# Two unrolled layers with constant waits in a two-layer attention, SSD and mixture-of-experts kernel

## What is computed

```
h = rms_norm(x, norm1_g[i])
proj = h @ w_in[i]            # q | k | v | z | xbc | dt | gate_a | gate_m
ya = diff_attention(q, k, v, lam, rel_bias)    # 8 heads, two softmax maps each
ym = ssd_mixer(z, xbc, dt_raw, ...)            # conv of 5, chunked scan both ways
merged = sigmoid(gate_a) * (ya @ w_attn_out) + sigmoid(gate_m) * (ym @ w_ssm_out)
x = x + merged @ w_out[i]
hn = rms_norm(x, norm2_g[i])
x = x + hier_moe(hn, ...)     # top 1 of 4 groups, top 2 of its 8 experts, 32 experts of width 512
```

## Time and profile before

| | |
|---|---|
| median of three runs | 1922.25 us |
| the profiled execution, its own time | 1922.67 us |
| its span in the trace | 1920.6 us |
| PE busy | 1749.7 us, 91% |
| granted TensorE clock, mean | 0.968 |

### The profile page before, as it was taken

One profiled execution on the slowest core, in us unless ns is written; L12 is line 12 of the kernel. 1 busy time (PEld: TensorE's weight loads), 2 busy tenths in 40 slices (PEclk: granted clock), 3 DMA queues, 4 the chain that ended last, 5 costly groups with the idle time before them and its releaser, 6 DMA issues.

```text
span 1920.6 us, 27786 instructions
## 1 busy us (share of the span) xinstructions
PE 1749.7 (91%) x9070; PEld 1094.1 (57%) x9070; DVE 710.0 (37%) x1363; ACT 656.6 (34%) x1318; POOL 666.4 (35%) x536
## 2 busy tenths in 40 slices
PE   6999999998799999998769999999987999999997
PEld 5889766787444343343358897667864433443432
DVE  5528576423321221221255285674232212222211
ACT  4565555754111111111145665557441111111110
POOL 6688655796000000000056886557950000000000
PEclk9999899998899999999989998999988999999999
DMA  6444211455699999999924442114557999999995
GB/s 254 169 176 174 91 45 45 176 221 218 279 421 426 428 427 428 428 428 427 395 97 158 176 176 89 45 45 176 233 205 291 427 428 427 427 429 427 428 427 251
DMA packets 39770, 528.87 MB, mean 275 GB/s; under 512 B 4248, under 2 KB 7064, under 8 KB 7872
## 3 DMA queue, kind: packets, MB, share of 16 engines
q1 hardware_dynamic: 39584, 526.89, 66.7%
q0 software_dynamic: 32, 0.02, 0.0%
HBM read 525.82 MB, written 1.06 MB: 274 GB/s over the span
## 4 chain that ended last, share of the span: by engine, by line
PE 49%; issue 32%; POOL 8%; DMA 5%; DVE 4%; ACT 1%; SPq 0%; POOLq 0%; DVEq 0%; ACTq 0%
PE PS L1038 9%; POOL view L1946 8%; PE PS L721 5%; PE PS L723 5%; PE PS L722 5%; PE PS L1069 5%; DMA view<-in_w_exp_up_dram 5%; PE PS L855 2%; PE PS L815 2%; PE PS L816 2%; PE PS L817 2%; DVE view L1588 2%; PE PS L1019 2%; PE PS L890 1%; PE PS L1004 1%
## 5 line engine op out<-in xcount | busy, mean ns | idle before, releaser
L1946 POOL TENSOR_TENSOR view<-view,view 128x512 fp32r<-128x512 f32 x448 | 578.6, 1314 | 650.1 <-ACT view L1158 645.3
L1038 PE MATMUL PS<-view,view 128*64 128x512 f32 x2048 | 447.7, 593 | 26.7 <-DMA view<-in_w_exp_up_dram 18.1
L1158 ACT ACTIVATE view<-view 128x512 fp32r<-128x512 f32 x448 | 273.6, 628 | 201.0 <-PE PS L723 189.8
L1038 PEld LDWEIGHTS PS<-view,view 128*64 128x64 f32 x2048 | 146.8, 137 | 321.5 <-issue 321.4
L721 PE MATMUL PS<-view,view 128*128 128x512 f32 x704 | 296.3, 421 | 8.9 <-POOL view L1946 7.2
L723 PE MATMUL PS<-view,view 128*128 128x512 f32 x704 | 276.0, 392 | 0.0
L722 PE MATMUL PS<-view,view 128*128 128x512 f32 x704 | 275.8, 392 | 0.0
L1069 PE MATMUL PS<-view,view 128*64 128x512 f32 x1024 | 231.9, 606 | 1.0 <-ACT view L1407 1.0
L1839 DVE TENSOR_TENSOR view<-PS,view 128x512 f32<-128x512 f32 x32 | 22.1, 692 | 486.7 <-PE PS L1019 421.3
L721 PEld LDWEIGHTS PS<-view,view 128*128 128x128 f32 x704 | 133.6, 190 | 47.4 <-POOL view L1946 12.6
L722 PEld LDWEIGHTS PS<-view,view 128*128 128x128 f32 x704 | 133.6, 190 | 32.8 <-issue 8.2
(11 more groups left out here) (241 smaller groups left out, 2055.8 us busy)
## 6 DMA issues: line engine op xcount, KB each, us to landing
view<-in_w_exp_gate_dram SPq DMA_DIRECT2D x64, 2048.0 KB, 19.9
view<-in_w_exp_up_dram SPq DMA_DIRECT2D x64, 2048.0 KB, 22.7
view<-in_w_exp_down_dram SPq DMA_DIRECT2D x64, 2048.0 KB, 25.8
view<-in_w_mix_dram SPq DMA_DIRECT2D x56, 2048.0 KB, 8.0
view<-bias_table SPq DMA_DIRECT2D x2, 1536.0 KB, 11.4
view<-in_x_dram SPq DMA_DIRECT2D x1, 1024.0 KB, 5.2
out_dram<-view SPq DMA_DIRECT2D x1, 1024.0 KB, 5.3
dtw<-in_w_dt_dram SPq DMA_DIRECT2D x2, 256.0 KB, 11.0
```

The source lines that it names most:

```text
L1038: ins = pe.matmul(bank(ph, name, j)[e * CAP:(e + 1) * CAP, :], xgT2[h % 2][:, k, at + e * CAP:at + (e + 1) * CAP], slot8[expert_block(j, k ...
L1158: nc.scalar.activation(highs(chunk), weights(slot8, chunk), ACT.Copy).then_inc(*high_ready.up(ph))
L1946: g_.tensor_tensor(weights(low8, chunk), weights(slot8, chunk), highs(chunk), ALU.subtract).then_inc(*low_ready.up(ph))
```

## The change

PE, ACT, DVE, POOL and SP each have both layers written out one after the other, so all wait values are constants. Each layer has its own semaphores for the overflow passes, so the Else branch with its 27 credits is gone. The layer's vectors have one buffer for each layer, SP loads into it directly, and the copy at line 1490 is gone. ACT and DVE load the flag after pair 2 of the expert stage, SP after its load number 16; PE loads it where it did. DVE works out the next layer's head scales after pair 8 of the expert stage. ACT's squares at the start of layer 1 wait for the last additions to X one half of the tokens at a time.

```
@@ Signal.at
-        v = ph.layer * ((self.mixer + UNITS * self.unit) * self.step) + (k * self.step + self.credit)
+        v = k * self.step + self.credit
         if ph.unit is not None:
-            v = v + ph.unit * (self.unit * self.step) + self.mixer * self.step
-        return self.sem, v
+            return self.sem, v + ph.unit * (self.unit * self.step)
+        return self.sem, v + ph.layer * (self.mixer * self.step)
@@ buffers and signals
-        vnext = sb("vnext", [P, R1 + R2])
-        vcol = sb("vcol", [P, R1 + R2])
+        vcols = [sb(f"vcol{i}", [P, R1 + R2]) for i in range(DEPTH)]
-        over_S = sig("over_S", 0, 1)
+        over_S = in_layers("over_S", 0, 1)
...
@@ SP, behind load number 16 of the expert stage
-                    if n == 2 * SLOTS and not last:
+                    if n == 2 * SLOTS:
                         sp.wait_ge(*flag_ready.at(ph, 1))
-                        vectors(l + 1, Phase(l + 1))
+                        sp.sem_inc(s_anchor, 1)
+                        over = sp.value_load(flag[0:1, 0:1], min_val=0, max_val=1)
+                        if not last:
+                            vectors(l + 1, Phase(l + 1))
@@ ACT, start of a layer
-                act.wait_ge(s_x, 16)
-                act.wait_ge(*drained[5].at(ph, 0))
-                act.wait_ge(*drained[6].at(ph, 0))
+                if l == 0:
+                    act.wait_ge(s_x, 16)
                 for t in range(TT):
+                    if l:
+                        for n in range(2):
+                            act.wait_ge(*out_of(Phase(l - 1), "s", ALL_PAIRS - 1, t, n))
                     nc.scalar.activation(sq[:, t * D:(t + 1) * D], X[:, t, :], ACT.Square,
                                          accum_out=small[:, t:t + 1]).then_inc(*sumsq.up(ph))
                 cast(ph, 0, HIGHS)
-                act.wait_ge(*cols_ready.at(ph, 1))
+                act.wait_ge(*small_in.at(ph, 3))
@@ ACT, expert stage
                     rest(ph, j)
+                    if j == 2:
+                        act.wait_ge(*flag_ready.at(ph, 1))
+                        act.sem_inc(s_anchor, 1)
+                        over = act.value_load(flag[0:1, 0:1], min_val=0, max_val=1)
@@ DVE, start of a layer
-                dve.wait_ge(*small_in.at(ph, 3))
-                v.tensor_copy(vcol[:, :], vnext[:, :]).then_inc(*cols_ready.up(ph))
-                dve.wait_ge(*cols_ready.at(ph, 1))
-                link(v.tensor_tensor(small[:, 12:13], vcol[:, GHN:GHN + 1], lamc[:, 1, ds(l, 1)], ALU.mult))
-                for i in range(2):
-                    link(v.tensor_tensor(bc_lq[:, 2 * i, :], bc_lq[:, 2 * i, :], bc_lq[:, 2 * i + 1, :], ALU.mult))
-                    link(v.tensor_reduce(small[:, 6 + i:7 + i], bc_lq[:, 2 * i, :], AX, ALU.add))
+                vcol = vcols[l]
+                if l == 0:
+                    head_scales(ph)
                 norm_rows(1, 2, 2)
@@ DVE, expert stage and end of a layer
                     scaled_low(ph, j)
+                    if j == 2:
+                        dve.wait_ge(*flag_ready.at(ph, 1))
+                        dve.sem_inc(s_anchor, 1)
+                        over = dve.value_load(flag[0:1, 0:1], min_val=0, max_val=1)
+                    if j == ALL_PAIRS // 2 and l + 1 < DEPTH:
+                        head_scales(Phase(l + 1))
                 add(ph, ALL_PAIRS - 1)
-                dve.wait_ge(*flag_ready.at(ph, 1))
-                dve.sem_inc(s_anchor, 1)
-                over = dve.value_load(flag[0:1, 0:1], min_val=0, max_val=1)
                 with dve.If(over > 0):
...
-                with dve.Else():
-                    for b in range(8):
-                        dve.sem_inc(over_filled[b].sem, UNITS * UNIT_FILLS[b])
...
@@ the end of PE, ACT, DVE and POOL each
-            with dve.Fori(0, DEPTH) as l:
+            for l in range(DEPTH):
                 layer(l)
```

More of the change, by code:

```diff
@@ L1131, in unit @@
                     scatter(ph, PAIRS - 1, t)
-                check_made(ph, {f"filled{b}": over_filled[b] for b in range(8)})
-            with pe.Fori(0, DEPTH) as l:
+                check_made(ph, {f"filled{b}": over_filled[ph.layer][b] for b in range(8)})
+            for l in range(DEPTH):
                 layer(l)
@@ L1424, in unit @@
                     rest(ph, j)
-                check_made(ph, {"yeh": over_yeh})
-            with act.Fori(0, DEPTH) as l:
+                check_made(ph, {"yeh": over_yeh[ph.layer]})
+            for l in range(DEPTH):
                 layer(l)
@@ L2004, in layer @@
                 check_made(ph, {"low_ready": low_ready, "xd": xd_ready, "xD": xD_ready, "yo": yo_ready, "z": z_done})
-            with pool.Fori(0, DEPTH) as l:
+            for l in range(DEPTH):
                 layer(l)
```

113 lines of the change are left out of this document (58 added, 55 removed).

## The result

The changed kernel takes 1910.94 us, the median of six executions (1909.7 to 1912.75). The kernel before takes 1922.03 beside it (six, 1917.93 to 1923.25). The ratio is 0.995, with a 95% interval of 0.9939 to 0.9962. So it is faster by 11.1 us, where I had forecast 6.3, and the time lies just under the low end of my range (1911.0). My bound for "the forecast is wrong", a gain over 10 us, is passed.

The account below looks back on a forecast made before the run. PE was taken to bound the mixer and weight transfers the late expert stage, leaving the gap between the layers to gain. 1922.67 - 6.9 + 0.9 - 0.3 = 1916.4, or 1916.0 us against the median; range 1911.0 to 1919.0.

Parts of the forecast that it names:

- Between the layers: DVE's chain starts 10.86 us earlier, but POOL's four operations block four of its 13 steps: gain 6.9 us; chance 0.52.
- The rival in which POOL doesn't block DVE: Between the layers: DVE's steps run beside POOL unhindered, gain 10.9 us, time 1911.9, or 1909.5 at best; chance 0.22.
- the one of late code: Between the layers: forward branches cost like the loop's, ACT squares from 958.8, 1.6 us less gain, 1917.6; chance 0.14.
- the first rival: Between the layers: POOL does not hold up DVE's chain; range 1909.5 to 1913.5 us, chance 0.22.
- Table load: Layer 1's fifth block: the 1.28 us load returns ahead of the exponential, before a PE stall of 1.49; plus 0.9 us.
- Constant waits: Both layers' dependent steps: wait values need no computing, but this lies under the step before; zero, with 0 to 1.5 kept.
- The end: Kernel's end: without DVE's credits and branch all engines can part earlier; minus 0.3 us.
- The clock.: At PE's restart between the layers: full clock returns the same distance behind the earlier restart; no gain and no loss.
- a rival that makes the kernel slower: Longer half clock after PE's restart (2.7 us) and after the deeper fifth-block stall in layer 1 (5.1): 1923.8; chance 0.08.

Follow-up runs that it names:

- casts_first: Changed kernel with ACT's first four casts of layer 1 ahead of its squares, so POOL's operations run before DVE's chain: 1906.98 us, ratio 0.9938.
- squares_wait: Changed kernel with the old wait put back, both squares of layer 1 waiting for all of X: 1912.6 us, ratio 0.9952.
- before_unrolled: Kernel before with only both layers written out on all engines; credits, copy, head scales and flag loads stay between the layers: 1912.38 us, ratio 0.9961.
- after_again: Changed kernel measured on another occasion, no edit: 1911.23 us, ratio 0.9954.
- after_exp_early: Changed kernel with a one-column exponential on ACT at layer 1's start, so the table load falls in idle time: 1909.06 us, ratio 0.9937.
- pool_held: Changed kernel with POOL's addition in the scan's last unit held until DVE has made the map PE waits for: 1909.97 us, ratio 0.9941.
- before_router_busy: Kernel before with 26 unread products on PE in its wait ahead of the router's transpositions: 1915.67 us, ratio 0.998.
- after_router_busy: Changed kernel with 26 unread products on PE in its wait ahead of the router's transpositions: 1911.3 us, ratio 0.9953.
- casts_router: Changed kernel with the edits of casts_first and after_router_busy together: 1903.38 us, ratio 0.9911.

## Why the prediction was right, and where it was wrong

**Between the layers: right, to 0.1 us.** This is the mechanism of the forecast, and it was not luck. The second square's place, the sums, three steps free, four blocked, PE at 10.6: all as reckoned. casts_first and squares_wait moved the cause and the effect followed. The rival in which POOL doesn't block DVE is refuted by the same rows. So is the one of late code: ACT's second square begins 0.09 us after the last addition ends (954.65 + 0.69 to 955.43), and DVE's branch takes 0.07 us. The time alone would have misled: 1910.9 lies in the range that I gave to the first rival, 1909.5 to 1913.5, and its mechanism is the one that the rows refute.

**Table load: right in size, wrong in place.** Forecast +0.9, measured +0.83. I had put it on the stall at the block's end, 1.49 before; that one is 1.48 now. The load fell on the one ahead of it (0.31 to 1.14). It goes with the layers written out, as before_unrolled shows, and not with any other part of the change.

**Constant waits: I took zero, and the net is small, but not for my reason.** In a chain the steps are 0.20 apart in both kernels, as I said. But where an engine has several waits behind a step, their values were computed after it. At the third block DVE's multiplication began 0.39 us behind its chain before the change, and 0.04 behind it now. Before:

```profile
67.05 0.17 DVE L1463 SCALAR_TENSOR_TENSOR stat<-stat 128x16 f32<-128x16 f32 x1
...
67.61 1.29 DVE L1512 TENSOR_TENSOR view<-PS,stat 128x512 f32<-128x512 f32 x2 [0.39 <-DVE stat L1463]
```

After:

```profile
67.84 0.17 DVE L1484 SCALAR_TENSOR_TENSOR stat<-stat 128x16 f32<-128x16 f32 x1
68.05 1.29 DVE L1529 TENSOR_TENSOR view<-PS,stat 128x512 f32<-128x512 f32 x2
```

PE's waits at two such places, between starts, fell from 1.94 to 1.77 and from 1.45 to 0.82, the one ahead of the scan from 4.18 to 3.80, and the one ahead of the router from 7.68 to 7.50: 0.17 + 0.63 + 0.38 + 0.18 = 1.36 us a layer. before_unrolled has the same waits to 0.01 us, so they come with the layers written out. The collision of POOL and DVE took 1.04 back. Net 0.3 a layer, 0.6 in all, inside the 0 to 1.5 that I kept. The collision is the very mechanism that I had reckoned with between the layers, and I had not asked where else constant waits would bring POOL forward onto DVE.

**The end: 0.3 forecast, 0.4 to 0.6 measured** (7.3 to 6.9, 6.8 and 6.7).

**The fixed part.** 6.9 + 0.6 + 0.4 - 0.8, less 0.3 for a stall late in layer 1 that rose from 0.93 to 1.27, whose cause I did not follow, make 6.8 us. My sum was 6.3, and the lowest executions of the two kernels are 6.7 apart.

**The step that failed is "The clock."** I took it at one place, PE's restart, with no gain and no loss, and had it elsewhere only as a rival that makes the kernel slower. The profiled execution of the kernel before, against which the sum was made, had the router's products at 1.2 GHz in both layers, and the stretch at 7.0 us for 32 small products was there to be read. Whether they meet 1.2 or 2.4 GHz changes from execution to execution, and layer 1 is 2.0 us longer for it: from the last mixer product to the last of the layer, 492.8, 492.9 and 493.0 us in the three traces at half clock (before, after_again, after_exp_early), 490.8 to 491.1 in the five others without unread products (the changed kernel, before_unrolled, squares_wait, pool_held, casts_first). In layer 0 the two traces at half clock have 495.6 and 495.2 us (before, pool_held) and the other six 491.5 to 494.1, so there it is worth 1 to 4. Of the 12.1 us between the two profiled executions, 5.0 lie in the router's products. (In the expectation of after_again I called the changed kernel's 4.62 us a time at 2.4 GHz. It is mixed, at 0.78 of the clock; all at 2.4 GHz the products take 3.7.)

By my own criterion, "if the mixer or the expert stage gets shorter by over 1.5 us, the constant waits were worth more than I say", the constant waits should have been the cause. In the profiled executions they were not. The stretch was shorter, but by the clock. The 1.5 us was a good alarm with the wrong name on it.

**What stays open.** Why the changed kernel meets the router at half clock less often than the kernel before does. In the eight traces without unread products, the half clock that begins in the router's wait lasted 30.7 us where it began 2.4 to 3.2 us behind the start of the last mixer product (four layers, both of the kernel before among them), 6.8 us where it began 3.5 to 4.8 behind (eleven layers) and 27.3 at 5.2 (one). With one trace of the kernel before I can't say whether it falls early by chance there, or whether the change moves it; the rival that the change itself does so is untested. One thing narrows the spread of the changed kernel. In after_again and after_exp_early, layer 1 met the router at half clock, but its half clock at the start of the scan had lasted 6.8 us and not 10.2. The stage from the scan to the last mixer product takes 246.6 to 247.0 us in three traces with 6.8 (these two and before_unrolled) and 248.5 to 248.6 in three with 10.2 (the changed kernel, squares_wait, casts_first). So some 1.5 of the 2.0 us had been won ahead of the router.

Medians differ by 9.3 to 11.1 us, lowest times by 6.7, and no execution of the changed kernel in 11 lies where both layers at half clock would put it, 4 us above its lowest. With unread products in the router's wait of both (before_router_busy and after_router_busy) the medians are 4.4 us apart, less than 6.8. In their traces the clock still favours the changed kernel, 3.5 us for the router's products of each layer against 4.6 and 5.1, but routing and experts of layer 1 took 477.9 us against 473.4. So there are some microseconds in the stage that the transfers pace which nothing here explains.

## What to carry to other kernels

Before you sum up a change against one profiled execution, look for stages whose clock is at half behind a wait of PE, and ask whether the next execution would find them so: such a stage moves the time by whole microseconds from one execution to the next. Unread products in PE's waits are a way to hold the clock, where operands and bank are idle: those ahead of the scan were worth 5.8 us between medians (1903.38 to 1897.58). Measure each time, though: those ahead of the router were worth 4.8 us in the kernel before and nothing in the changed one. And when something makes an engine earlier by a few hundredths, check the places where GpSimd and VectorE start together: the order of two starts was worth 1.0 us.

## What the runs showed of the hardware that I had not expected

POOL's start 0.03 us ahead of DVE's instead of 0.06 behind made a DVE step of 0.22 us last 1.25. Not all of DVE's small operations are held: in before_unrolled the reduction at 962.51, beside POOL's last operation between the layers, took 0.22 us, between a copy of 0.87 and products of 0.93 to 1.25.

The clock's fall in one and the same wait of 7 us came 2.4 to 5.2 us after the start of PE's last product, and 32 products of 36 columns took 3.7 to 3.8 us at 2.4 GHz (after_router_busy), 7.0 at 1.2, and 4.1 to 5.6 where the level changed among them. After a wait of only 3.5 us the clock was at half for the next 10.2 us (6.8 in layer 1 of some traces), though PE was busy for 8.8 of 10 us (casts_router), and 14 products in that wait kept it up.
